# The first value units of a decoder block, taken chunk by chunk on TensorE, with squares, gates and value copies in another order

## The reference

```python
h = rmsnorm(x, g_mix[i])
proj = h @ w_in[i]
q, k, v, f_logit, gb, gc_in, xc, g_attn, g_conv = jnp.split(proj, IN_SPLITS, axis=-1)
attn = forgetting_attention(q, k, v, f_logit + b_f[i])      # uses cumsum of log_sigmoid(f_logit)
...
x = x + merged @ w_out[i]
x = x + peer(rmsnorm(x, g_ffn[i]), ...)                     # 128 x 128 single-neuron experts
ple_gate = jax.nn.sigmoid(rmsnorm(x, g_ple[i]) @ w_ple_gate[i])
x = x + ple_gate * (p[i] @ w_ple_proj[i])
```

## Time and profile before

| what | value |
|---|---|
| median of 3 runs | 1730.43 us (1730.11 to 1730.67) |
| profiled execution, its own time | 1730.14 us |
| span of its trace | 1728.4 us |
| PE busy | 1721.9 us |
| DVE, ACT, POOL busy | 1331.1, 725.3, 941.6 us |

### The profile page before, as it was taken

The page is one execution under the profiler, slowest core; times in us unless marked ns, Lnnn a source line. Parts: engine busy times, 40 slices in busy tenths (PEclk is TensorE's granted clock), DMA queues, the critical chain, the costliest instruction groups (busy, mean ns, idle before and its releaser), DMA issues.

```text
span 1728.4 us, 25620 instructions
## 1 busy us (share of the span) xinstructions
PE 1721.9 (100%) x9288; PEld 1493.0 (86%) x9288; DVE 1331.1 (77%) x2393; ACT 725.3 (42%) x1116; POOL 941.6 (54%) x743
## 2 busy tenths in 40 slices
PE   9999999999999999999999999999999999999998
PEld 7888888888888888899999999888888888888887
DVE  7666322468799999999999998446888888888874
ACT  7644322443332222334333433444444444444454
POOL 6433344443347777777777777236666656564200
PEclk9999999999999999999999999999999999999999
DMA  6322332348764444254444444769999999999721
GB/s 209 106 66 73 107 125 92 115 182 314 253 232 150 150 146 154 68 164 161 159 153 160 158 161 160 253 212 338 377 372 380 368 377 368 379 364 382 286 86 50
DMA packets 156382, 363.35 MB, mean 210 GB/s; under 512 B 31680, under 2 KB 72640, under 8 KB 156128
## 3 DMA queue, kind: packets, MB, share of 16 engines
q1 hardware_dynamic: 102224, 259.56, 43.5%
q0 software_dynamic: 34816, 67.41, 10.9%
q10 hardware_dynamic: 19216, 34.74, 5.5%
HBM read 300.54 MB, written 61.01 MB: 209 GB/s over the span
## 4 chain that ended last, share of the span: by engine, by line
PE 96%; DVE 2%; ACT 1%; issue 1%; DMA 1%; POOL 0%; SPq 0%; DVEq 0%; ACTq 0%; POOLq 0%
PE pair L682 18%; PE pair L684 18%; PE pair L683 18%; PE pair L927 18%; PE pair L950 7%; PE pair L949 7%; PE pair L951 7%; PE pair L803 1%; PE pair L891 1%; DMA raw<-stream 1%; PE pair L794 0%; PE pair L1034 0%; PE pair L825 0%; POOL wl L606 0%; PE pair L826 0%
## 5 line engine op out<-in xcount | busy, mean ns | idle before, releaser
L636 POOL DMA_INDIRECT gates<-gate_val,gate_at x384 | 444.4, 1157 | 151.5 <-issue 112.0
L606 POOL TENSOR_TENSOR wl<-raw,wh 128x1024 fp32r<-128x1024 f32 x85 | 205.8, 2429 | 286.4 <-ACT wh L1137 275.2
L1137 ACT ACTIVATE wh<-raw 128x1024 fp32r<-128x1024 f32 x266 | 280.1, 1058 | 171.2 <-PE pair L684 152.6
L682 PE MATMUL pair<-wh,act_h 128*128 128x512 f32 x768 | 299.3, 390 | 0.0
L683 PE MATMUL pair<-wl,act_h 128*128 128x512 f32 x768 | 299.2, 390 | 0.0
L684 PE MATMUL pair<-wh,act_l 128*128 128x512 f32 x768 | 299.2, 390 | 0.0
L1815 DVE TENSOR_TENSOR wl<-raw,wh 128x1024 fp32r<-128x1024 f32 x182 | 220.9, 1218 | 42.3 <-ACT wh L1137 41.8
L655 POOL DMA_INDIRECT picked<-score_dram,score_at x128 | 149.9, 1171 | 173.6 <-PE pair L684 111.5
L682 PE MATMUL pair<-hh,wh 128*128 128x512 f32 x456 | 182.3, 400 | 0.0
L684 PE MATMUL pair<-hh,wl 128*128 128x512 f32 x456 | 178.4, 391 | 0.0
L683 PE MATMUL pair<-hl,wh 128*128 128x512 f32 x456 | 177.8, 390 | 0.0
(11 more groups left out here) (307 smaller groups left out, 3513.5 us busy)
## 6 DMA issues: line engine op xcount, KB each, us to landing
raw<-stream SPq DMA_DIRECT2D x337, 512.0 KB, 4.1
score_dram<-gout ACTq DMA_DIRECT2D x128, 256.0 KB, 2.3
gates<-zeros SPq DMA_DIRECT2D x48, 512.0 KB, 6.2
score_in<-score_dram SPq DMA_DIRECT2D x128, 192.0 KB, 6.2
gate<-gates SPq DMA_DIRECT2D x128, 192.0 KB, 6.6
gates<-gate_val,gate_at POOLq DMA_INDIRECT x384
x<-xT SPq DMA_DIRECT2D x7, 512.0 KB, 4.7
picked<-score_dram,score_at POOLq DMA_INDIRECT x128, 5.7
```

What stands on the lines that cost most here:

```text
L606: nc.gpsimd.tensor_tensor(wl[:, n % SL, :], raw[:, n % RAW, :], wh[:, n % SL, :].bitcast(F32), ALU.subtract).then_inc(lo_done, 1)
L636: nc.gpsimd.indirect_dma_start(gate_list, bass.IndirectOffsetOnAxis(ap=gate_at[:, r, k:k + 1], axis=0), gate_val[:, r, k:k + 1], None).the ...
L682: nc.tensor.matmul(out, ah, bh, start=start, stop=False)
L1137: nc.scalar.activation(wh[:, n % SL, :], raw[:, n % RAW, :], ACT.Copy).then_inc(hi_done, 1)
```

## The change

PE issues 11 warm-up products in place of 18. Unit 0 goes through `first_values`: all three kinds of product of chunk 0, then all of chunk 1; its low part is made by POOL in two halves, the first after the first half of the high part (semaphore `first_half`, which takes the place of `hi_first`). `norm_sums` moves from before to behind the low products of unit 1. On ACT the three small DMAs move from the start to behind unit 0's high part, and the squares of chunks 0 and 1 move behind the high part of unit 1; DVE makes four low parts of x first and then all eight sums. Half of the forget-gate products move in between the first chunks of `project(U_MIX, 0)`, and the copies of the value banks move in between the last normed chunks on ACT.

```diff
@@ -600,6 +600,14 @@
 
                 if low_by_dve(n):
                     return
+                if n == 0:
+                    pool.wait_ge(first_half, 1)
+                    nc.gpsimd.tensor_tensor(wl[:, 0, 0:T], raw[:, 0, 0:T], wh[:, 0, 0:T].bitcast(F32),
+                                            ALU.subtract).then_inc(first_half, 1)
+                    pool.wait_ge(hi_done, 1)
+                    nc.gpsimd.tensor_tensor(wl[:, 0, T:], raw[:, 0, T:], wh[:, 0, T:].bitcast(F32),
+                                            ALU.subtract).then_inc(lo_done, 1)
+                    return
                 pool.wait_ge(hi_done, n + 1)
                 if n == 2:
                     pool.wait_ge(diag_ready, TT)
@@ -743,28 +751,57 @@
                     nc.tensor.matmul(psum[bank][:, 0:P], ones[:], ones[:], start=True, stop=True)
 
             pe.wait_ge(consts, 2)
-            keep_warm(7, 18)
+            def first_values():
+
+                for c in range(2):
+                    cols = slice(c * CW, (c + 1) * CW)
+                    if c == 0:
+                        pe.wait_ge(first_half, 1)
+                    else:
+                        pe.wait_ge(hi_done, 1)
+                    for part, weights in ((hh, wh), (hl, wh), (hh, wl)):
+                        if part is hl:
+                            pe.wait_ge(xl_ready, c + 1)
+                        elif weights is wh:
+                            pe.wait_ge(xh_ready, c + 1)
+                        elif c == 0:
+                            pe.wait_ge(first_half, 2)
+                        else:
+                            wait_low(pe, 0)
+                        for tt in range(TT):
+                            last = nc.tensor.matmul(psum[tt][:], part[:, c, tt * P:(tt + 1) * P], weights[:, 0, cols],
+                                                    start=c == 0 and part is hh and weights is wh, stop=False)
+                last.then_inc(unit_used, 1)
+
+            keep_warm(7, 11)
             pe.wait_ge(consts2, 6)
-            pe.wait_ge(hi_first, 1)
-            for j in range(4):
+            first_values()
+            for j in range(1, 4):
                 values(j, hh, wh, True, False)
                 if j == 2:
                     norm_rows(0)
                 values(j, hl, wh, False, False)
+                wait_low(pe, U_V + j)
+                values(j, hh, wl, False, True).then_inc(unit_used, 1)
                 if j == 1:
                     norm_sums(0)
-                wait_low(pe, U_V + j)
-                values(j, hh, wl, False, True).then_inc(unit_used, 1)
 
             pe.wait_ge(wf_split, 2)
-            for c in range(DC):
+            def forget_gates(c):
+
                 pe.wait_ge(h_ready, c + 1)
                 nc.tensor.matmul(psum[6][0:2 * HEADS, :], wf_parts[:, c, :], hh[:, c, :], start=c == 0, stop=False)
-                last = nc.tensor.matmul(psum[6][0:2 * HEADS, :], wf_parts[:, c, :], hl[:, c, :], start=False, stop=c == DC - 1)
-            last.then_inc(f_ready, 1)
-
+                return nc.tensor.matmul(psum[6][0:2 * HEADS, :], wf_parts[:, c, :], hl[:, c, :], start=False, stop=c == DC - 1)
+
+            for c in range(DC // 2):
+                forget_gates(c)
             pe.wait_ge(v_out, 1)
-            project(U_MIX, 0)
+            for c in range(DC):
+                if c < DC // 2:
+                    last = forget_gates(DC // 2 + c)
+                    if c == DC // 2 - 1:
+                        last.then_inc(f_ready, 1)
+                project(U_MIX, 0, c, c + 1)
 
             pe.wait_ge(f_out, 1)
             for tt in range(TT):
@@ -1128,8 +1165,6 @@
         def _(act):
 
             act.dma_start(gain[:], gains).then_inc(gain_in, 16)
-            for dst, src in ((wf, w_f), (bfb, b_f), (convw, conv_w)):
-                act.dma_start(dst[:], src).then_inc(const_in, 16)
 
             def high(n):
 
@@ -1160,23 +1195,25 @@
 
                 nc.scalar.activation(high_part[:, c, :], x[:, c, :], ACT.Copy, scale=gain[:, k, c:c + 1]).then_inc(xh_ready, 1)
 
-            act.wait_ge(consts, 6)
+            act.wait_ge(consts, 3)
             nc.scalar.activation(spare[:, 0:1], eps[:], ACT.Sqrt)
             act.wait_ge(gain_in, 16)
             act.wait_ge(x_first, 16)
             plain_high(0, hh, 0)
             act.wait_ge(raw_first, 16)
-            nc.scalar.activation(wh[:, 0, 0:T], raw[:, 0, 0:T], ACT.Copy).then_inc(hi_first, 1)
+            nc.scalar.activation(wh[:, 0, 0:T], raw[:, 0, 0:T], ACT.Copy).then_inc(first_half, 1)
             act.wait_ge(x_in[0], 16)
             plain_high(0, hh, 1)
             act.wait_ge(raw_in[0], 16)
             nc.scalar.activation(wh[:, 0, T:], raw[:, 0, T:], ACT.Copy).then_inc(hi_done, 1)
-            square(0, 0)
-            square(0, 1)
+            for dst, src in ((wf, w_f), (bfb, b_f), (convw, conv_w)):
+                act.dma_start(dst[:], src).then_inc(const_in, 16)
             act.wait_ge(x_in[1], 16)
             plain_high(0, hh, 2)
             plain_high(0, hh, 3)
             high(1)
+            square(0, 0)
+            square(0, 1)
             square(0, 2)
             square(0, 3)
             for i in range(2, 4):
@@ -1188,17 +1225,25 @@
             high(2)
             root(0)
             high(3)
+            def values_out(tt):
+
+                nc.scalar.activation(v_sb[:, tt, :], psum[tt][:], ACT.Copy, scale=factor[:, tt:tt + 1]).then_inc(v_out, 1)
+
             act.wait_ge(const_in, 48)
             nc.scalar.activation(wf_h, wf[:], ACT.Copy).then_inc(wf_split, 1)
             for c in range(DC):
                 if c % 2 == 0:
                     act.wait_ge(unit_used, U_V + c // 2 + 1)
+                if c == 6:
+                    act.wait_ge(diag_ready, TT)
+                    values_out(0)
+                elif c == 7:
+                    values_out(1)
+                    values_out(2)
                 normed_high(0, c)
                 if c < 4:
                     high(4 + c)
-            act.wait_ge(diag_ready, TT)
-            for tt in range(TT):
-                nc.scalar.activation(v_sb[:, tt, :], psum[tt][:], ACT.Copy, scale=factor[:, tt:tt + 1]).then_inc(v_out, 1)
+            values_out(3)
             for n in range(3):
                 next_high(U_V + n)
             next_high(U_V + 3)
@@ -1647,12 +1692,9 @@
                                                in1=high_part[:, c, :].bitcast(F32), op0=ALU.mult,
                                                op1=ALU.subtract).then_inc(xl_ready, 1)
 
-            for i in range(2):
-                plain_low(0, hh, hl, 2 * i)
-                plain_low(0, hh, hl, 2 * i + 1)
-                add_square(0, 2 * i)
-                add_square(0, 2 * i + 1)
-            for c in range(4, DC):
+            for c in range(4):
+                plain_low(0, hh, hl, c)
+            for c in range(DC):
                 add_square(0, c)
             for c in range(4, DC):
                 plain_low(0, hh, hl, c)
```

More of the change, by code:

```diff
@@ L354, in peer_block_kernel @@
         raw_first = sem("raw_first")
-        hi_first = sem("hi_first")
+        first_half = sem("first_half")
         gain_in = sem("gain_in")
```

## The result

The changed kernel takes 1734.3 us in the median of 13 runs (1731.91 to 1735.1); the kernel before, in 13 runs beside them, 1730.38 (1729.98 to 1731.05). The ratio is 1.0022 with a 95% interval of 1.0014 to 1.0029: slower by 3.9 us. The interval rules out no change at all, but doesn't rule out a change smaller than 0.2% (3.5 us). The median lies above the range of the forecast (1728.9 to 1733.9). The runs spread over 3.2 us where those of before spread over 1.1, and they sort by the granted clock that each printed: 1734.69 on average for the seven with 0.998, 1733.43 for the five with 0.999, 1731.91 for the one with 1.000. Only 0.998 sets them apart: of the runs of before that stand beside the experiments, 38 of 98 print 0.999 too and none prints less (one more, at a clock of 0.77, took 3147 us and is not counted).

The account below looks back on a forecast made before the run. PE's work was taken as the bound, with DVE's gate chain deciding the running sums. PE comes 1.0 us late, DVE 2.0: 1730.14 + 2.0 = 1732.1, the median 0.3 above, so 1732.4 us; range 1728.9 to 1733.9.

Parts of the forecast that it names:

- The step that failed: PE ahead of unit 2: waits for the late sums and high part, 2.4 us idle, 1.0 us late.
- a rival with a chance of 0.13: Clock falls in PE's gap, 17.4 to 20.75: 6 us at the lower level, 3.0 lost, 1735.3 us; chance 0.13.
- the term that was put at nothing: Gap ahead of unit 2: the forecast's own case adds no time for a fall of the clock.
- The sign that the prediction had named for itself: PE after 20 us: 512-column products more than 0.4 us apart would show the forecast wrong.
- The opening: PE before unit 2: unit 0 starts at 5.9, unit 1 ends at 17.4; a head start of 1.4 us at most.
- The squares: ACT and DVE behind unit 1's high part: two sums added, 2 x 0.80 = 1.6 us later, taking back the head start.
- the bound of 0.3: ACT's opening: fewer small transfers competing with the first pieces bring it forward by 0.3 us at most; taken as nothing.
- The DMA issues: Three on ACT in the place of two squares: no delay, or 0.45 us if they wait; taken as nothing.
- The forecast's 1.0 us: Delay of unit 2's start on PE: 20.75 against 19.74 before.
- Unit 7's transfer: Waits for the buffer unit 3's low part frees: high part from 28.83 to 30.4, normed chunks 4 to 6 +1.6 us.
- The value copies: On ACT, 0.6 us each, two ahead of chunk 7: 0.4 of DVE's 2.0 us delay at the last normed chunk.
- The gate chain: DVE from last normed chunk to the running sums: shifts without a break, ends at 49.2 against 47.21, 2.0 us late.

Follow-up runs that it names:

- the gap filled: The changed kernel with 3 warm-up products ahead of `norm_sums` and 6 behind it, so PE is busy ahead of unit 2: 1732.60 us.
- 18 warm-up products: The changed kernel with all 18 warm-up products in place of 11: 1732.73 us.
- squares back: The changed kernel with the squares of chunks 0 and 1 and their two sums put back ahead of unit 1's high part: 1731.26 us.
- squares and copies back: The changed kernel with squares, sums and value copies put back and the cast of `tri` moved to the start of DVE: 1731.23 us.
- the copies back: The changed kernel with all four value copies behind the last normed chunk again: 1733.25 us.
- the early cast: The changed kernel with the cast of `tri` moved to the start of DVE: 1732.39 us.

## Why the prediction was wrong

**The step that failed.** "PE is now 1.0 us late, with 2.4 us of idle time in the gap": the gap was priced as a delay and nothing more, and the fall of the clock was left to a rival with a chance of 0.13 because "a gap of this size may be harmless". It isn't. The changed kernel's profile shows 6.8 us at the lower level and 3.0 us lost on unit 2, and filling the gap takes 1.5 to 1.7 us off the median with no other edit. In the prediction's sum the term that was put at nothing is the clock's, and it measured 3.0 us on PE in the profile. The sign that the prediction had named for itself came: 512-column products more than 0.4 us apart after 20 us. The rival's own price was good: 6 us at the lower level, 3.0 us lost, 1735.3 us; the profiled execution has 6.8, 3.0 and 1735.10. But the 6 us were taken over from the opening, four other profiles show a stretch of 3.4, and this is the slowest of 13 runs, so a part of the agreement is luck. That no row of before shows a fall was true, and no evidence: its longest wait behind the opening was 0.4 us, so it could not have shown one.

**The opening** was right: unit 0 at 5.81 (5.9 forecast), unit 1's end at 16.8 (17.4), since the clock rose sooner: four products take 1.03 us from 5.81 on, where three slow ones alone would take 1.3. That it gives nothing by itself was right as well: with 11 products alone the old kernel gains nothing that can be measured.

**The squares** were right in kind and in size. Forecast was 1.6 us more between unit 1's high part and unit 2's; measured is 9.28 - 7.66 = 1.62 us, and 9.28 again with the gap filled. The times themselves are all some 0.6 us earlier than forecast (first sum 11.34 for 12.0, eighth sum's end 17.61 for 18.25), because unit 1's high part started 0.67 us early, twice the bound of 0.3. The DMA issues cost ACT nothing (the first runs at 7.08 beside an activation at 7.07), and the second half of unit 0 came 0.55 us sooner. That the moved small transfers are the reason is not shown: the old kernel with 11 warm-up products, which issues them at the start, has unit 1's high part at 9.74 as well, and the profiles of all kernels spread from 9.74 to 10.52. So unit 2 was late by less than forecast, 20.22 against 19.97. The forecast's 1.0 us also has a slip of 0.2 in it: 19.74 is the start of unit 2's first weight load, its first product starts at 19.97.

**Unit 7's transfer**: in the changed kernel hidden behind the slow clock, but with the gap filled ACT waits 0.89 us for it and rounds at 30.21 (forecast 30.4).

**The value copies**: 0.4 us forecast, 0.40 measured in DVE's wait for chunk 7 with the gap filled. In the changed kernel it is 0.60 + 0.95, because PE is so late that the first copy, too, stands in the way of chunk 6. That they pay for themselves as soon as the gate chain is early was not foreseen: the prediction has them as a cost alone, and that holds only while DVE binds.

**The gate chain**: I let it shift as a block. It doesn't: the cast of `tri` took 2.51 us where it took 1.89, +0.6, since it met POOL's work at another point. Two errors offset each other: with the gap filled, the last normed chunk ends at 36.41 (36.75 forecast), the chain behind it takes 12.9 us (12.4), the running sums start at 49.41 (49.27, PE waiting 1.57 for 1.25) and the median is 1732.60 (1732.4), 2.5 over its runs of before (2.0). For that kernel, in which the clock holds, the forecast is near, and partly by that luck.

**The split of the 3.9 us.** By medians: 1.5 to 1.7 for the clock (filled gap against none), and 2.2 to 2.5 for the chain behind the squares, which holds the late sums, the two copies and the cast. Each of these figures has an interval of at least 1.6 us to either side. How the last three divide is known from traces only.

## What to carry to other kernels

A wait on PE is not only its length: where PE waits among light work, here for 1.3 us and more, put fillers there, or price the products behind it at the lower clock. Two operations moved behind a unit's preparation delay everything that queues behind them on that engine by their partner's step, here 2 x 0.80 us on DVE, so a head start of PE is worth nothing until the engine that feeds it has it too. And put a DVE cast where POOL is idle, then look at the cast behind it: here the next one met POOL instead, and the old kernel gained nothing.

## What was not expected of the hardware

- The clock fell after one wait of 1.34 us and about 0.9 us of one-column products (the old kernel with the squares moved), after 1.51 us behind such products (18 warm-up products), and held with 1.17 us behind them (squares back) and with 0.58 us (squares and copies back). From the last full product before to the first behind, that is 2.4 and 2.5 us where it fell and 2.1 and 1.5 where it held, each in one profile. The fall need not come in the wait: in four of the five profiles that show it PE was back at full products, for 0.2 to 1.3 us. The Trainium skill ("TensorE: Matmul & The Clock Gate", section on the HAM clock gate) says that an idle PE returns to 1.2 GHz; the traces agree on the level. The time at the lower level was 3.4 us in the profiles with 18 products, with the copies back, with the early cast and with the old kernel's squares moved, and 6.8 us in the changed kernel's.
- A DVE cast to fp32r that begins while POOL is in a `wl` subtraction ends with it or just behind it. For `logf_h` that is so in all ten profiles in which it begins there, 0.03 to 0.05 us behind POOL's end, as 46.72 against 46.68; it took 0.24 to 1.97 us so, and 0.18 in the four profiles in which POOL was idle. The cast of `tri` takes 0.50 us at 2.95, and 1.89 to 2.53 beside POOL in eight profiles, ending 0.3 us behind it. The Trainium skill ("GPSIMD Engine Reference", section "Specifications") says that the two engines share their way to SBUF and contend when DVE runs in a two-port mode or has two inputs in SBUF. The trace agrees for these casts, with up to a whole POOL operation as the price (in which mode they run no trace shows), while `hl<-x,gain,hh` with its two inputs went from 0.75 us to no more than 1.11 in the kernel before.
